# Operand tiles of the first and last feed-forward network placed 1280 (one set 1288) bytes apart

## What is computed

```
layer 0:  x += 0.5 swiglu(norm x)   x += mamba2(norm x)      x += 0.5 swiglu(norm x)   x += gated embedding
          shared K, V from x
layer 1:  x += 0.5 swiglu(norm x)   x += attention(norm x)   x += 0.5 swiglu(norm x)   x += gated embedding
swiglu(x) = (silu(x @ wi_gate) * (x @ wi_up)) @ wo         wi: 1024 x 5632, wo: 2816 x 1024
```

## Time and profile before

| | us |
|---|---|
| three runs | 1187.78, 1188.85, 1189.05 |
| the profiled execution, its own time | 1188.74 |
| its span, first to last instruction | 1186.9 |
| TensorE matmul busy | 1174.9 (99%) |
| VectorE busy | 866.4 (73%) |
| ScalarE busy | 698.7 (59%) |
| GpSimd busy | 246.2 (21%) |

### The profile page before, as it was taken

One profiled execution on the slowest core, in us unless ns is written; L12 is line 12 of the kernel. 1 busy time (PEld: TensorE's weight loads), 2 busy tenths in 40 slices (PEclk: granted clock), 3 DMA queues, 4 the chain that ended last, 5 costly groups with the idle time before them and its releaser, 6 DMA issues.

```text
span 1186.9 us, 26623 instructions
## 1 busy us (share of the span) xinstructions
PE 1174.9 (99%) x9823; PEld 1153.3 (97%) x9823; DVE 866.4 (73%) x1377; ACT 698.7 (59%) x1149; POOL 246.2 (21%) x352
## 2 busy tenths in 40 slices
PE   9999999999999999999999999999999999999998
PEld 8999999999999899999999999999999899999998
DVE  7766645999899858767745987788468777776447
ACT  6445435777786747555546765555368765444345
POOL 1000001422221202122344333232026310000001
PEclk9999999999999999999999999999999999999999
DMA  8765554755445375866886677656743346555552
GB/s 288 253 205 181 183 184 143 256 180 202 162 157 193 113 220 179 329 214 247 283 299 232 213 269 280 226 166 237 261 150 108 106 163 209 186 184 178 179 181 86
DMA packets 63297, 239.90 MB, mean 202 GB/s; under 512 B 7672, under 2 KB 9632, under 8 KB 58848
## 3 DMA queue, kind: packets, MB, share of 16 engines
q1 hardware_dynamic: 56880, 197.83, 49.8%
q0 software_dynamic: 6064, 40.66, 9.4%
q10 hardware_dynamic: 288, 0.54, 0.2%
HBM read 226.87 MB, written 13.39 MB: 202 GB/s over the span
## 4 chain that ended last, share of the span: by engine, by line
PE 87%; DVE 7%; ACT 3%; DMA 2%; issue 1%; POOL 0%; SPq 0%; DVEq 0%; ACTq 0%; POOLq 0%
PE bank L509 28%; PE bank L510 27%; PE bank L511 27%; DVE wlo L1576 1%; DMA raw<-weights 1%; DVE xact L1850 1%; DMA xact<-stat_rows 1%; ACT whi L1098 1%; DVE xl L1595 1%; PE bank L881 1%; PE bank L907 0%; PE bank L886 0%; ACT under L1494 0%; PE bank L687 0%; DVE zs L1976 0%
## 5 line engine op out<-in xcount | busy, mean ns | idle before, releaser
L1576 DVE TENSOR_TENSOR wlo<-raw,whi 128x1024 fp32r<-128x1024 f32 x367 | 456.0, 1246 | 236.9 <-ACT whi L1098 235.5
L509 PE MATMUL bank<-xh,whi 128*128 128x264 f32 x2008 | 576.5, 287 | 1.9 <-DVE zs L1623 0.8
L510 PE MATMUL bank<-xl,whi 128*128 128x264 f32 x2008 | 569.6, 284 | 0.0
L511 PE MATMUL bank<-xh,wlo 128*128 128x264 f32 x2008 | 569.3, 284 | 0.0
L1098 ACT ACTIVATE whi<-raw 128x1024 fp32r<-128x1024 f32 x367 | 385.5, 1054 | 242.4 <-PE bank L511 225.1
L509 PEld LDWEIGHTS bank<-xh,whi 128*128 128x128 f32 x2008 | 378.6, 189 | 5.0 <-DVE wlo L1576 1.8
L510 PEld LDWEIGHTS bank<-xl,whi 128*128 128x128 f32 x2008 | 378.8, 189 | 0.8
L511 PEld LDWEIGHTS bank<-xh,wlo 128*128 128x128 f32 x2008 | 376.9, 188 | 0.0
L509 PE MATMUL bank<-hh,whi 128*128 (+1 forms) x896 | 255.9, 286 | 1.8 <-DVE hl L1960 1.7
L511 PE MATMUL bank<-hh,wlo 128*128 (+1 forms) x896 | 255.0, 285 | 0.0
L510 PE MATMUL bank<-hl,whi 128*128 (+1 forms) x896 | 254.7, 284 | 0.0
(11 more groups left out here) (335 smaller groups left out, 1007.2 us busy)
## 6 DMA issues: line engine op xcount, KB each, us to landing
raw<-weights SPq DMA_DIRECT2D x367, 512.0 KB, 3.5
under<-ssm POOLq DMA_DIRECT2D x8, 1024.0 KB, 7.1
xact<-ssm POOLq DMA_DIRECT2D x8, 1024.0 KB, 7.4
out_ssm_s<-xact POOLq DMA_DIRECT2D x8, 1024.0 KB, 6.0
xact<-dtx_rows POOLq DMA_DIRECT2D x5, 1024.0 KB, 10.7
zs<-dtx_rows POOLq DMA_DIRECT2D x2, 1024.0 KB, 14.1
x<-xT SPq DMA_DIRECT2D x4, 264.0 KB, 5.6
xact<-stat_rows POOLq DMA_DIRECT2D x2, 528.0 KB, 7.5
```

The costliest lines, as they stand in the source:

```text
L509: pe.matmul(out, whi[:, w, c], rh, start=start, stop=False)
L510: pe.matmul(out, whi[:, w, c], rl, start=False, stop=False)
L511: return pe.matmul(out, wlo[:, w, c], rh, start=False, stop=stop)
L1576: dve.tensor_tensor(wlo[:, s, :], raw[:, s, :], whi[:, s, :].bitcast(F32), ALU.subtract).then_inc(lo_ready, 1)
```

## The change

Two sets of operand tiles are laid over the region that starts at 99456. The first network uses the first set, the last network the second. Arithmetic, number and order of the instructions stay; the tiles still hold 264 columns, but their distance grows from 1056 bytes to `pitch` x 4 bytes. By the same rule for addresses the places are:

| tiles | first set (f1i0, f1o0) | second set (f2i1, f2o1) |
|---|---|---|
| `hhw` | 99488, pitch 1288: residues 160, 168, ... (22 tiles) | 99552, pitch 1280: all 224 |
| `hlw` | 127904, pitch 1288: residues 160, 168, ... | 127712, pitch 1280: all 224 |
| `xhw` | 156384, pitch 1280: all 224 | 155872, pitch 1280: all 224 |
| `xlw` | 166624, pitch 1280: all 224 | 166112, pitch 1280: all 224 |

`xhw` and `xlw` of the second set lie over the place from which K and V are stored, so ScalarE waits for `kv_out` before it writes them.

```diff
+WIDE_FIRST, WIDE = 322, 320
...
+        wide = {}
+        for layer, (pitch, ahead_, between_, behind) in enumerate(((WIDE_FIRST, 8, 16, 32), (WIDE, 24, 0, 0))):
+            with ExitStack() as room:
+                place = lambda name, shape, dt=F32R: room.enter_context(nc.sbuf_tensor(f"{name}{layer}", [P] + shape, dt))
+                place("ahead", [ahead_], F32)
+                hhw = place("hhw", [FT, pitch])
+                if between_:
+                    place("between", [between_], F32)
+                hlw = place("hlw", [FT, pitch])
+                if behind:
+                    place("behind", [behind], F32)
+                wide[layer] = [t[:, :, 0:N] for t in (hhw, hlw, place("xhw", [KT, WIDE]), place("xlw", [KT, WIDE]))]
+        (hh_a, hl_a, xh_a, xl_a), (hh_b, hl_b, xh_b, xl_b) = wide[0], wide[1]
...
+        OUTER = {"f1o0": (hh_a, hl_a), "f2o1": (hh_b, hl_b)}
...
-            ffn_in("f1i0", None)
+            ffn_in("f1i0", None, rh=xh_a, rl=xl_a)
...
-            ffn_in("f2i1", 4)
+            ffn_in("f2i1", 4, rh=xh_b, rl=xl_b)
...
+                highs, lows = OUTER.get(stage, (hh, hl))
+                rh, rl = (highs[:, kt, :], lows[:, kt, :]) if isinstance(kt, int) else (
...
-            split_x(G_F2 + 8, 4, "o", 8)
+            act.wait_ge(kv_out, 64)
+            split_x(G_F2 + 8, 4, "o", 8, xh=xh_b)
...
-            add_b("o", 8, 1.0, G_F2 + 8, "f2i1")
+            add_b("o", 8, 1.0, G_F2 + 8, "f2i1", xh_b, xl_b)
```

More of the change, by code:

```diff
@@ L589, in first_units @@
                     mm.then_inc(unit_used, 2)
-                    unit_a(stage, 0, 2)
+                    unit_a(stage, 0, 2, rh=rh, rl=rl)
                     sums(stage)
-                    unit_a(stage, 0, 3)
+                    unit_a(stage, 0, 3, rh=rh, rl=rl)
                     return
@@ L748, in unit_b @@
                 pe.wait_ge(hl_ready, hready)
-                rh, rl = (hh[:, kt, :], hl[:, kt, :]) if isinstance(kt, int) else (
-                    hh[:, bass.ds(kt, 1), :].rearrange("p a n -> p (a n)"), hl[:, bass.ds(kt, 1), :].rearrange("p a n -> p (a n)"))
+                highs, lows = OUTER.get(stage, (hh, hl))
+                rh, rl = (highs[:, kt, :], lows[:, kt, :]) if isinstance(kt, int) else (
+                    highs[:, bass.ds(kt, 1), :].rearrange("p a n -> p (a n)"), lows[:, bass.ds(kt, 1), :].rearrange("p a n -> p (a n)"))
                 for m in order:
@@ L797, in stage_b @@
                 pe.wait_ge(hl_ready, h0_ + n)
+                highs, lows = OUTER.get(stage, (hh, hl))
                 for m in range(KT):
                     for j in (n - 2, n - 1):
-                        mm = split_products(bank[m][:, 0:N], (U0[stage] + j) % RING, m, hh[:, j, :], hl[:, j, :], False, j == n - 1)
+                        mm = split_products(bank[m][:, 0:N], (U0[stage] + j) % RING, m, highs[:, j, :], lows[:, j, :], False, j == n - 1)
                     if m < KT - 1:
@@ L1140, in split_tile, with split_x @@
                 square_x(m)
-            def split_x(gain, b_stage, stage=None, n=0, table=ACT.Sqrt):
+            def split_x(gain, b_stage, stage=None, n=0, table=ACT.Sqrt, xh=xh):
                 act.preload_act_table(table)
@@ L1146, in split_x @@
                     act.wait_ge(b_free, 8 * b_stage + m + 1)
-                    split_tile(m, gain)
+                    split_tile(m, gain, xh)
                 for j in range(max(n - 2, 0), n):
@@ L1162, in round_h @@
                     act.wait_ge(h_ready, FT * ffn + 2 * i + p + 1)
-                    dst = hh[:, 2 * i + p, :] if isinstance(i, int) else hh[:, bass.ds(2 * i + p, 1), :].rearrange("p a n -> p (a n)")
+                    highs = OUTER.get(out, (hh, hl))[0]
+                    dst = highs[:, 2 * i + p, :] if isinstance(i, int) else highs[:, bass.ds(2 * i + p, 1), :].rearrange("p a n -> p (a n)")
                     act.activation(dst, gu[:, 2 * p + 1, :], ACT.Copy).then_inc(hh_ready, 1)
@@ L1239, in _ @@
                     act.wait_ge(x_pair[m // 2], 16)
-                act.activation(xh[:, m, :], x[:, m, :], ACT.Copy, scale=gain0[:, m:m + 1]).then_inc(xh_ready, 1)
+                act.activation(xh_a[:, m, :], x[:, m, :], ACT.Copy, scale=gain0[:, m:m + 1]).then_inc(xh_ready, 1)
                 if m == 1:
@@ L1596, in low_x, with add_b @@
                                          in1=xh[:, m, :].bitcast(F32), op0=ALU.mult, op1=ALU.subtract).then_inc(xl_ready, 1)
-            def add_b(stage, n, scale, gain, after):
+            def add_b(stage, n, scale, gain, after, xh=xh, xl=xl):
                 b = BSTAGE[stage]
@@ L1608, in add_b @@
                     if m > 0:
-                        low_x(m - 1, gain, XREADY[after])
-                low_x(7, gain, XREADY[after])
+                        low_x(m - 1, gain, XREADY[after], xh, xl)
+                low_x(7, gain, XREADY[after], xh, xl)
                 for j in range(n - 2, n):
@@ L1639, in low_h @@
                     one = (lambda a: a[:, 2 * i + p, :]) if isinstance(i, int) else (lambda a: a[:, bass.ds(2 * i + p, 1), :].rearrange("p a n -> p (a n)"))
-                    dve.tensor_tensor(one(hl), gu[:, 2 * p + 1, :], one(hh).bitcast(F32), ALU.subtract).then_inc(hl_ready, 1)
+                    highs, lows = OUTER.get(out, (hh, hl))
+                    dve.tensor_tensor(one(lows), gu[:, 2 * p + 1, :], one(highs).bitcast(F32), ALU.subtract).then_inc(hl_ready, 1)
                 if stage == "f1i0":
@@ L1779, in _ @@
                 dve.wait_ge(xh_ready, m + 1)
-                dve.scalar_tensor_tensor(out=xl[:, m, :], in0=x[:, m, :], scalar=gain0[:, m:m + 1], in1=xh[:, m, :].bitcast(F32),
+                dve.scalar_tensor_tensor(out=xl_a[:, m, :], in0=x[:, m, :], scalar=gain0[:, m:m + 1], in1=xh_a[:, m, :].bitcast(F32),
                                          op0=ALU.mult, op1=ALU.subtract).then_inc(xl_ready, 1)
```

## The result

The changed kernel takes 1195.28 us, the median of twelve runs, against 1188.84 us before (twelve runs, 1187.78 to 1190.33). The ratio is 1.0043, with a 95% interval from 1.0032 to 1.0053: it is slower by 0.4%. The runs are not scattered around the median, though. Five lie between 1190.67 and 1191.14 us, none between that and 1195.09, and seven from 1195.09 to 1197.77.

A forecast was written before the change was run, and what follows sets the result against it. TensorE's matmul pace was taken to bound the kernel; 1.84 us (f1i0, f2i1) + 0.1 (f2o1) + 0.16 (f1o0) gave +2.1 us on 1188.74, so 1190.8 us, with a range from 1185.0 to 1193.0 us.

The forecast's parts named there:

- The bound: Whole kernel: TensorE's matmuls busy for 99% of the span at full clock, so only their pace can change the time.
- f1i0 and f2i1 at 121.7 ns: Input stages, 1056 matmuls each: pace from 120.83 to 121.7 ns at constant residue 224, +0.92 us each, +1.84 in both.
- The step taken on trust: f1i0 and f2i1: an a-unit with constant residue behaves as a b-unit with constant residue, despite the differing PSUM bank.
- The bound of 121.9 ns for a constant residue: f1i0 and f2i1: upper bound from the settled pace of residue 224, +1.1 us a stage.
- f2o1: Output stage of the last network, all at 224: 121.5 to 121.7 ns, +0.1 us; stage 64.3 us instead of 64.16.
- Reading linearly between multiples of 32: f1o0, pitch 1288: sixteen tiles read off between neighbouring rows; 22 units add up to 64.3 us, +0.16 us.
- The slower rival: f1o0: starts off multiples of 32 bytes cost at least the worst multiple, +1.2 us; sum +3.6 us, 1192.3 us; chance 0.27.
- one of the signs: f1o0 timeline: stage between 64.0 and 64.6 us, longest units where the residue passes 0 (tiles 12 to 14).
- The faster rival: All four stages: constant residue settles better, at 120.0 ns everywhere; -3.4 us, 1185.3 us; chance 0.26.
- The wait for `kv_out`: ScalarE, before the table load and first `xh` of f2i1: stores landed 25 us earlier, cost 0.
- The case without effect: All stages: pace follows something else with the tiles' period, so paces stay and time is 1188.8 us; chance 0.07.
- The other stages: Sign in the changed kernel's timeline: stages other than f1i0, f2i1, f1o0 and f2o1 keep their lengths to 0.1 us.

The follow-up runs named there:

- e9: Changed kernel with one small extra matmul of 32, 64, 128 or 200 columns in turn ahead of each unit of f2i1's loop; run once, 1194.66 us.
- e11: Changed kernel with f1o0's tiles at pitch 1296 instead of 1288, f1i0's tiles 512 bytes further on; one execution 1189.70 us.
- e1: Changed kernel again, no edit; ten runs 1188.36 to 1197.88 us, ratio 1.0026, profiled execution 1196.61 us.
- e4: Changed kernel with pitch 1280 and residue 96 for all tiles in both networks; 1186.59 us, ratio 0.9972.
- e12: Repeat of pitch 1280 and residue 96 for all tiles in both networks; 1185.79 us, ratio 0.9967.
- e6: Kernel before the change with its three weight buffers 32 bytes further on, moving tiles at their old residues; 1189.89 us, ratio 1.0001.
- e7: Changed kernel with pitch 1280 everywhere, residue 0 in the first network and 64 in the last; 1190.02 us, ratio 1.0003.
- e2: Changed kernel with only the first network changed, the last as before and without the `kv_out` wait; 1190.40 us, ratio 1.0015.
- e3: Changed kernel with only the last network changed, the first as before, `kv_out` wait kept; 1190.05 us, ratio 1.0002.
- e5: Changed kernel with only f1i0's input tiles moved from residue 224 to 96; 1189.49 us, ratio 1.0002.

## Why the prediction was wrong

It said +2.1 us and within 0.2%; measured is +6.4 us in the median, 1195.28 us where its range ends at 1193.0. Point by point:

- **The bound** (TensorE's pace and nothing else) holds: both groups have the same count, clock and idle time.
- **f1i0 and f2i1 at 121.7 ns** was met exactly, 121.67 in both, in the profiled execution. The step taken on trust, that an a-unit behaves as a b-unit, is right in f2i1, and in f1i0 in that execution: the pattern of four is the same, f2i1 and f2o1 agree at 121.67, and neither the bank nor the multiples of 256 show.
- **The step that failed** is the one before it: a residue was given *one* settled pace, read from units that were all entered from the same neighbour, tile 2 at 192. It is a set of paces, of which the entry picks one (e9, e11). While tiles rotate, every tile is a new entry, and the stage comes out the same (64.16 us in both b-stages of the earlier trace rows); with a constant residue the stage keeps to its end, for some 40 units, what the pause ahead of its loop led to. In f1i0 that pause differs between executions (0.23 to 0.34 us), in f2i1 it doesn't. The bound of 121.9 ns for a constant residue was therefore no bound; 126.67 exists, 5 ns x 1056 = 5.3 us. The term for f1i0, +0.92 us and at most +1.1, came to 135.47 - 130.10 = +5.4 us in e1, and seven of twelve runs have an f1i0 of that sort by their times.
- **f2o1**: 64.24 us, forecast 64.3. **f1o0**: 64.62 us, +0.46 where +0.16 was forecast. Reading linearly between multiples of 32 was mis-sized, since half of the new starts are off a 16-byte line. The slower rival came near this mechanism: it blamed starts off a multiple of 32, with +1.2 us, and e11 shows that starts on a multiple of 16 are cheap. The effect was worth 0.58 us against pitch 1296. A unit of f1o0 is 64.62 / 22 = 2.94 us long in the mean, just past the rival's mark of 2.93, but this did not decide: the lower group, which has it, is 1.8 to 2.3 us above before and so inside the band of 2.4 us. The longest units are not at residue 0 (tile 12) either, as one of the signs said; they are tiles 11 (248) and 15 (24), both off 16 bytes.
- **The faster rival** said that a constant residue might settle better, at 120.0. That is real too, for 96, 64, 0 and 128 and in e11 even for 224. Its sum of -3.4 us is what e4 and e12 measured at 96: -3.3 and -3.9 us by their ratios.
- **The wait for `kv_out`** cost 0, as worked out.
- **The case without effect**, a pace that follows something else with the period of the tiles, is excluded by e4, whose four stages changed pace with the residue, and by e6.
- **The other stages** were to keep their lengths to 0.1 us. sout didn't (50.1 to 52.7 us), so this sign could not be used as it stood.

What stays open: why the entry leads to one pace or another, how often each is met at a residue, and whether e7's upper runs are f1i0 at 123.3 ns. That the upper group of the change is f1i0 at 126.67 ns rests on one profiled execution, on e2 and e3, and on its absence in e5, on another chip; of the five executions profiled with f1i0 at 224 three have 121.67 ns, one 126.67 and one 120.0.

## What to carry to other kernels

Where the same matmul repeats at full clock without idle time, measure its pace to the ns, by unit, against the start of the moving tile modulo 256 relative to the weights' start; keep moving tiles on 16-byte starts. If you make that distance constant, take one for which every pace met is good (here 96, which is -32 from the weights), disturb the stream on purpose to look for others, and time it often: a pace that is read from tiles in rotation belongs to that rotation.

## What the runs showed that was not expected

A settled matmul stream can hold one of several paces for over 100 us at full clock: 120.0, 121.67 and 126.67 ns for 264 columns at the same starts modulo 256. The last two came with the very same addresses in f1i0, and 120.0 and 121.67 with the very same addresses in f2i1 (e9), there for one unit at a time. A small matmul of 32 to 200 columns is enough to change between two of them. Moving the weights by 32 bytes against the moving tiles moves the dear and the cheap units by one tile, so the pace depends on the place of both together. That it is TensorE's two reads, of weights and of moving tile, that meet is the likely reading, but no run separates them from the writes to `whi` and `wlo`, which moved as well. Here the trace goes against the Trainium skill, "SBUF — State Buffer", section "Who interferes with whom", by which these two reads of PE have independent ports and PE never waits on anyone: unit 4 went from 2.97 to 2.92 us and unit 5 from 2.92 to 2.96. The measurement decides. No constant residue has shown a settled mean below 120.0 ns.
